# Rows of the last five expert blocks kept in SBUF, the others added onto the tokens by DMA during the last blocks

## What is computed

```
mod = silu(c) @ w_ada + b_ada                    # 9 rows: 1 prompt, 8 sample groups
sh1, sc1, g1, sh2, sc2, g2 = split(mod, 6)       # 1024 columns each
...
h2 = x * (1 + sc2) + sh2
for e in 16 experts (each token takes 2 of them, weights gate[e]):
    he = silu(h2 @ w_e_gate[e]) * (h2 @ w_e_up[e])
    y  = y + gate[e] * (he @ w_e_down[e])
x = layer_norm(ALPHA * x + (1 + g2) * y, ln2_g, ln2_b)
```

## Time and profile before

| | us |
|---|---|
| median of 3 runs | 1105.62 |
| the runs | 1103.91 to 1107.01 |
| the profiled execution | 1110.89 |
| its span, first to last instruction | 1109.0 |
| PE busy in the span | 1009.2 |
| DVE busy | 492.8 |
| ACT busy | 186.2 |
| POOL busy | 253.0 |
| mean granted TensorE clock (1 is 2.4 GHz) | 0.948 |

### The profile page before, as it was taken

The page is one execution under the profiler, slowest core; times in us unless marked ns, Lnnn a source line. Parts: engine busy times, 40 slices in busy tenths (PEclk is TensorE's granted clock), DMA queues, the critical chain, the costliest instruction groups (busy, mean ns, idle before and its releaser), DMA issues. The chain is left out here.

```text
span 1109.0 us, 22156 instructions
## 1 busy us (share of the span) xinstructions
PE 1009.2 (91%) x8966; PEld 676.4 (61%) x8966; DVE 492.8 (44%) x1281; ACT 186.2 (17%) x441; POOL 253.0 (23%) x287
## 2 busy tenths in 40 slices
PE   4999999998999999999999999987999999998930
PEld 3777777455876766667777764565655555554510
DVE  2122999972356888855104004677133011010117
ACT  2110112113122212221111110111111111111103
POOL 0000005445121113222325430000221221211133
PEclk8998999999798999999999999986999999999975
DMA  9955645452515206114081317142969899999856
GB/s 307 300 112 157 181 153 204 142 194 78 196 29 162 67 15 193 31 46 113 11 211 36 114 52 300 66 180 96 367 252 417 324 377 392 421 414 419 323 155 121
DMA packets 93733, 214.23 MB, mean 193 GB/s; under 512 B 23465, under 2 KB 48304, under 8 KB 89534
## 3 DMA queue, kind: packets, MB, share of 16 engines
q1 hardware_dynamic: 78388, 186.20, 47.0%
q0 software_dynamic: 6400, 19.01, 5.8%
q10 hardware_dynamic: 8849, 7.64, 2.5%
HBM read 200.46 MB, written 16.92 MB: 196 GB/s over the span
## 5 line engine op out<-in xcount | busy, mean ns | idle before, releaser
L1747 PE MATMUL bank<-arena 128*128 128x288 f32 (+6 forms) x1778 | 444.1, 406 | 6.5 <-issue 2.1
L1747 PEld LDWEIGHTS bank<-arena 128*128 128x128 f32 (+2 forms) x1778 | 321.3, 193 | 121.3 <-issue 45.9
L2138 PE MATMUL bank<-arena 128*32 128x256 f32 x3136 | 181.4, 382 | 8.5 <-issue 6.6
L2138 PEld LDWEIGHTS bank<-arena 128*32 128x32 f32 x3136 | 103.5, 109 | 78.4 <-issue 12.4
L1699 DVE TENSOR_TENSOR arena<-arena,bank 128x128 f32<-128x128 f32 x49 | 14.2, 289 | 229.5 <-ACT arena L1142 229.3
L914 POOL DMA_INDIRECT expert_rows<-arena,ints x49 | 47.7, 974 | 228.0 <-ACT arena L1153 228.0
L864 POOL TENSOR_SCALAR arena<-arena 128x288 f32<-128x288 f32 x48 | 45.3, 943 | 219.5 <-ACT arena L1104 219.5
L2157 PE MATMUL bank<-arena 128*32 128x256 f32 x1568 | 94.6, 381 | 0.0
L1215 DVE SCALAR_TENSOR_TENSOR arena<-arena 128x512 f32<-128x512 f32 x120 | 81.9, 741 | 0.0
L1761 PE MATMUL bank<-arena 128*128 128x288 f32 x256 | 69.2, 428 | 2.6 <-DVEq L1233 2.6
L1751 PE MATMUL bank<-arena 128*128 128x128 f32 (+7 forms) x315 | 51.7, 300 | 17.8 <-DMA arena<-constants 5.0
(11 more groups left out here) (282 smaller groups left out, 880.5 us busy)
## 6 DMA issues: line engine op xcount, KB each, us to landing
arena<-in_w_e_gate SPq DMA_DIRECT2D x16, 2048.0 KB, 11.0
arena<-in_w_e_up SPq DMA_DIRECT2D x16, 2048.0 KB, 16.3
arena<-in_w_e_down SPq DMA_DIRECT2D x16, 2048.0 KB, 21.4
arena<-in_w_ada SPq DMA_DIRECT2D x8, 2048.0 KB, 10.5
arena<-in_w_in SPq DMA_DIRECT2D x8, 2048.0 KB, 10.1
arena<-in_w_ada SPq DMA_DIRECT2D x8, 1024.0 KB, 11.6
arena<-in_x_prompt SPq DMA_DIRECT2D x8, 512.0 KB, 5.2
arena<-in_w_in SPq DMA_DIRECT2D x14, 256.0 KB, 8.2
```

What stands on the lines that cost most here:

```text
L1747: last = pe.matmul(out, a, b, start=k == 0, stop=k == len(pairs_) - 1)
L2138: last = pe.matmul(out, HG[:, g % 2, k, a:a + BLK], gate_up[i % 2][:, :, k, c * P:c * P + P], start=k == 0, stop=k == KT - 1)
```

## The change

- `y_d` and a second tensor `y2_d` (for the further rows) are set to zero at the beginning: POOL clears 128 x 512 and issues two DMAs of 1,280 rows x 4 KB from it, in step `("ada", 8)`, ahead of that step's own work.
- Only the columns of `mod` from g1 on are stored. For n of 10 and 11 (g2) POOL adds 1 to the bias first, one more instruction each.
- Per block POOL fetches the quarters of 1 + g2 that its rows need (`gate_rows`, an indirect DMA of 128 rows x 1 KB) two blocks ahead; DVE, not ACT, takes the result out of PSUM and multiplies by weight and gate in one instruction (`result_up`).
- Blocks 0 to 43 (`SENT` = 44) are scattered as before. Blocks 44 to 48 (`KEPT` = 5) stay in `YR`.
- `GAT`, its five loads and DVE's L1730 go away. In their place POOL adds `y_d` onto `X1` in SBUF with accumulating DMAs: five for the first rows, five for the second, each second one after its first has landed. They begin when block 45 is up.
- The kept blocks are added by PE: one-hot matrices built by DVE in blocks 21 to 25, then per tile 5 x 4 products of 32 x 128 by 32 x 256 into four PSUM banks; DVE's sum over the row reads `X1` and these banks.
- DVE starts the end part only after POOL's `further_added`, which follows POOL's last accumulating DMA and its 21 branch tests.
- The list of rows carries a conditioning row number with each place, decoded by a few small DVE instructions in `list_up`, `spread_up`.

```diff
+SENT = FIRST[NE - 2]
+KEPT = NBLK - SENT
...
             if kind == "ada":
                 n = key[1]
+                if n == 8:
+                    own.link(pool.memset(ZERO, 0.0))
+                    for rows in (y_d, y2_d):
+                        pool.dma_start(rows[0:2 * SLEN].rearrange("(p n) (h d) -> p (n h) d", p=P, d=512),
+                                       ZERO.unsqueeze(1).broadcast_to([P, 2 * SLEN * 2 // P, 512])).then_inc(ev("zeroed"), 16)
...
                 pool.wait_ge(ev("mod_raw"), n - 3)
                 pool.wait_ge(ev(bada_in(n)[0]), bada_in(n)[1])
+                if n >= 10:
+
+                    own.link(pool.tensor_scalar(bada_buf(n), bada_buf(n), 1.0, None, ALU.add))
                 pool.tensor_tensor(mod_buf(n), mod_buf(n), bada_buf(n), ALU.add).then_inc(ev("mod_row"), 1)
...
+        def gate_rows(d):
+
+            pool.indirect_dma_start(G2B[:, d % 2, :], None, gates, bass.IndirectOffsetOnAxis(ints[:, I_ROW + d:I_ROW + d + 1], 0)).then_inc(ev(f"g2_in{d % 2}"), 16)
+
+        def add_rows(t, second, src, sem_name):
+            a = t * P + SLEN * second
+            pool.dma_start(X1[0:rows_of(t), t, :], src[a:a + rows_of(t), :], accum_op=ALU.add).then_inc(ev(sem_name), 16)
+
+        def firsts(t):
+            add_rows(t, 0, y_d, f"pair_in{t}")
+
+        def seconds(t):
+            pool.wait_ge(ev(f"pair_in{t}"), 16)
+            add_rows(t, 1, y_d, f"pair_in{t}")
+
+        pool.wait_ge(ev("weights_up"), 1)
+        gate_rows(0)
+        gate_rows(1)
+        for d in range(NBLK - 2):
...
             pool.wait_ge(ev("yo_up"), d + 1)
-            pool.indirect_dma_start(quarters, bass.IndirectOffsetOnAxis(ints[:, I_DEST + d:I_DEST + d + 1], 0), YR[:, d % YRS, :], None).then_inc(stored(d)[0], 16)
+            if d < SENT:
+
+                pool.indirect_dma_start(quarters, bass.IndirectOffsetOnAxis(ints[:, I_DEST + d:I_DEST + d + 1], 0), YR[:, yr_of(d), :], None).then_inc(stored(d)[0], 16)
+            gate_rows(d + 2)
+            if d == SENT + 1:
+
+                for done_ in stored_by(SENT):
+                    pool.wait_ge(*done_)
+                firsts(0)
+                firsts(1)
+                seconds(0)
+        firsts(2)
+        seconds(1)
+        firsts(3)
+        seconds(2)
+        firsts(4)
+        seconds(3)
+        seconds(4)
...
+        pool.sem_inc(ev("further_added"), 1)
...
+        def result_up(d):
+
+            dve.wait_ge(ev("dn_full"), d + 1)
+            if YRS <= d < SENT:
+                dve.wait_ge(*stored(d - YRS))
+            dve.wait_ge(ev(f"g2_in{d % 2}"), 16 * (d // 2 + 1))
+            stt(YR[:, yr_of(d), :], banks[6 + d % 2][:, 0:256], WBLK[:, d:d + 1], G2B[:, d % 2, :], ALU.mult, ALU.mult).then_inc(ev("yo_up"), 1)
...
+        dve.wait_ge(ev("further_added"), 1)
+        dve.wait_ge(ev("rows2_in"), 32)
         for t in range(NT):
-            n, a, m = rows_of(t), GAT[0:rows_of(t), t, :], TOTAL[0:rows_of(t), t:t + 1]
-            dve.wait_ge(ev(f"pair_in{t}"), 16)
-            link(tt_(a, a, BC2[0:n, 0 if t < 4 else 1, :], ALU.mult))
-            link(dve.tensor_tensor_reduce(out=a, in0=a, in1=X1[0:n, t, :], scale=1.0, scalar=0.0, op0=ALU.add, op1=ALU.add, accum_out=m))
...
+            dve.wait_ge(ev(f"pair_in{t}"), 32)
+            dve.wait_ge(ev("rows_summed"), t + 1)
+            by_quarter = x.rearrange("p (c f) -> p c f", c=4)
+            link(dve.tensor_tensor_reduce(out=by_quarter, in0=by_quarter, in1=sums[0:n], scale=1.0, scalar=0.0, op0=ALU.add, op1=ALU.add, accum_out=total))
...
+        for t in range(NT):
+            n = rows_of(t)
+            if t == 1:
+                pe.wait_ge(ev("yo_up"), NBLK)
+            if t >= 2:
+                pe.wait_ge(ev("row_mean"), t - 1)
+            for k in range(KEPT):
+                if t == 0:
+                    pe.wait_ge(ev("yo_up"), SENT + k + 1)
+                for c in range(4):
+                    rows = slice(BLK * c, BLK * c + BLK)
+                    last = pe.matmul(sum_banks(t)[0:n, c, :], OHT[k][rows, t, 0:n], YR[rows, YRS + k, :],
+                                     start=k == 0, stop=k == KEPT - 1)
+            last.then_inc(ev("rows_summed"), 1)
```

More of the change, by code:

```diff
@@ L151 @@
 A_YR = A_MG
[L152 removed]
+A_HEB = A_YR + (YRS + KEPT) * 256
 A_HETB = A_HEB + 3 * P
[L154 to L156 removed]
+A_G2 = A_HETB + 2 * P
+A_OHT = [A_BC + 6 * D, A_BC + 6 * D + SLEN, A_BC + 6 * D + 2 * SLEN, A_G2 + 512, A_HOT]
+assert len(A_OHT) >= KEPT and A_OHT[3] + SLEN <= A_MG + 4 * D and A_HOT + SLEN <= A_AE
 A_BC2 = A_HG + 2 * D
[L158 removed]
+assert A_BC2 + 2 * D <= A_BC + 6 * D
 A_O = A_RING
@@ L904, in _ @@
         quarters = y_d.rearrange("r (c f) -> (r c) f", c=4)
-        for d in range(NBLK):
-            if d == 0:
-                pool.wait_ge(ev("weights_up"), 1)
+        gates = mod_d.rearrange("r (k f) -> (r k) f", f=256)
+        def gate_rows(d):
[12 more added lines that the diff above has]
+        for d in range(NBLK - 2):
             for g in range(2, TILES):
@@ L1138, in _ @@
         act.activation(HG[:, 0, 4:8, :], quarter_tiles(banks[4]), ACT.Copy).then_inc(ev("gt_b"), 1)
-        for b in range(NBLK + 2):
-            if b < NBLK:
-                act.wait_ge(ev("hid_full"), b + 1)
-                act.activation(HEB[:, b % 3, :], banks[b % 3][:, 0:P], ACT.Silu).then_inc(ev("he_silu"), 1)
+        for b in range(NBLK):
+            act.wait_ge(ev("hid_full"), b + 1)
+            act.activation(HEB[:, b % 3, :], banks[b % 3][:, 0:P], ACT.Silu).then_inc(ev("he_silu"), 1)
             if b in tile_behind:
@@ L1169, in _ @@
             act.wait_ge(ev("row_mean"), t + 1)
-            act.activation(G[0:n, t % 2, :], GAT[0:n, t, :], ACT.Square, bias=NMEAN[0:n, t:t + 1], scale=1.0 / 32, accum_out=SQUARES[0:n, t:t + 1]).then_inc(ev("last_squares"), 1)
+            act.activation(G[0:n, t % 2, :], X1[0:n, t, :], ACT.Square, bias=NMEAN[0:n, t:t + 1], scale=1.0 / 32, accum_out=SQUARES[0:n, t:t + 1]).then_inc(ev("last_squares"), 1)
             act.wait_ge(ev("last_squares"), t + 1)
@@ L2204, in _ @@
         each_further(pe, nov, further)
+        with pe.If(nov > 0):
+            pe.wait_ge(ev("further_added"), 1)
+        pe.wait_ge(ev("he_ready"), NBLK)
+        pe.wait_ge(ev("het_up"), NBLK)
+        for t in range(NT):
+            n = rows_of(t)
+            if t == 1:
[10 more added lines that the diff above has]
+            last.then_inc(ev("rows_summed"), 1)
 def buckets():
@@ L2234, in constants @@
     c[:, K_STEP:K_STEP + NOV] = np.arange(NOV)[None, :]
-    c[:, K_DEST:K_DEST + 2 * NT] = p + P * np.arange(2 * NT)[None, :] + 1
+    token = p + P * np.arange(NT)[None, :]
+    row = np.where((token >= SEQ) & (token < NTOK), (token - SEQ) // ST + 1, 0)
+    c[:, K_DEST:K_DEST + 2 * NT] = p + P * np.arange(2 * NT)[None, :] + 1 + PLACES * np.concatenate([row, row], 1)
+    c[:, K_ROW:K_ROW + 1] = 12 + p // BLK
+    c[:, K_CND:K_CND + NB] = PLACES * np.arange(1, NB + 1)[None, :]
     c[:, K_LEFT:K_LEFT + 1] = p + 2 * SLEN + 1
```

162 lines of the change are left out of this document (88 added, 74 removed).

## The result

The changed kernel takes **1129.01 us** (median of 4 runs, 1124.39 to 1130.22); beside it the kernel before took 1104.76 (1103.57 to 1107.01). The ratio is 1.0202, with a 95% interval of 1.0171 to 1.0232. The profiled execution took 1130.22, its span is 1128.3, the mean granted clock 0.946. (PE is TensorE, ACT ScalarE, DVE VectorE, POOL GpSimd, SP SyncE.) The change is longer beyond doubt; whether by more than 2% the interval leaves open.

The account below looks back on a forecast made before the run. It took PE to bound the conditioning stretch, PE and transfers the expert blocks, and a chain of landings plus DVE's tiles the end. Terms 16.6 + 4 - 1.6 = +19 on 1105.6 gave 1125 us, range 1100 to 1138.

Parts of the forecast that it names:

- Zeroing, early: Conditioning stretch: POOL's small transfers land only behind the zeros, so PE is delayed by 16.6 us (ends +8.6 and +26.6).
- L: Conditioning stretch: the time the zeros land, taken as 282 (ends 274 and 292); PE resumes at L + 6.6.
- two landings that the prediction worked out: Conditioning stretch: zeros land at 282 by its own working, or at 278 by the Trainium skill's fit.
- 10 us or more: Conditioning stretch, sign of the forecast: PE idle this long between 270 and 290.
- Blocks: Expert blocks: fetched gate rows add bytes where DMA is full, +4 us (ends 0 and 9).
- DVE seldom waits: Expert blocks: fetches are issued two blocks (11 us) ahead and land after 6.8, so DVE rarely waits for them.
- End: After the blocks: DVE starts 4.5 us later, then its tiles and tail take 6.2 less; sum -1.6 (ends -17, +7).
- small transfers aren't held up: Rival, conditioning stretch: only shared bandwidth and added POOL instructions cost, +6 there, 1114 in all; chance 0.16.
- the full overlap: Rival, end: accumulating DMAs reach the plain rate and finish with the last block, end 17 us earlier; chance 0.14.
- slow accumulation: Rival, end: accumulating DMAs into SBUF cost 3.5 us each, 1134 in all; chance 0.08.
- hidden slack: Rival, early stretch: it has unseen slack, the rest as forecast, 1105 to 1108; chance 0.08.
- serial products: Rival, end: kept blocks' products run one after another, 8.5 us per tile, 1141 in all; chance 0.04.

Follow-up runs that it names:

- no fetches: The changed kernel with gate rows fetched for blocks 0 and 1 only and reused for all others; 1124.44 us, ratio 1.0154 to the kernel before.
- the kernel with four buffers: The changed kernel with gate rows fetched four blocks ahead in four buffers instead of two; 1127.32 us, ratio 1.0196 to the kernel before.
- the second profile of before: The kernel before, unchanged, profiled once more, on the third group's chip; 1109.14 us, span 1107.3.
- mended: The changed kernel with zeroing from SP's queue, bias instructions ahead of the raw-row wait, DVE's and POOL's single tests, spread transfers; 1109.55 us, ratio 1.0023.
- the kernel with the transfers spread: The changed kernel with DVE testing for further tiles, plus accumulating DMAs spread two each at blocks 44, 45, 46, four behind; 1122.10 us, ratio 1.0145.
- one test: The kernel with the transfers spread, plus POOL's 21 branches put inside one test for further tiles; 1127.76 us, ratio 1.0182 to the kernel before.
- each fetch twice: The changed kernel with each gate-row fetch done twice, the second copy into a spare place nobody reads; 1173.37 us, ratio 1.0586.

## Why the prediction was right

It said 1125 (1100 to 1138), slower at 0.76; it is 1129.0. By its steps, on the two spans:

1. **Zeroing, early: forecast +16.6, measured +15.4 at the gates.** The assumption that small transfers land only behind the zeros held: with the zeros on another queue the 25.9 us of a bias load are 5.9, and the gates come 13.6 us earlier. L was forecast at 282 and is 280.6, and PE resumes at L + 6.8 (forecast 6.6). Of the two landings that the prediction worked out, 282 and 278, the first was nearer. PE's idle time came out at 9.56 us, a little under the "10 us or more" that was to show it. What the sum left out: POOL's added issues delayed its root, a stall of 4.86 us for PE at 256.99 (1.38 before) that was absorbed, and the clock, which is 0.50 to about 306.
2. **Blocks: forecast +4, measured +6.4** (no fetches: 303.3 us, so about 5 are theirs). The mechanism fits, bytes where the transfers are full, though no run isolates the bytes; I counted from 915, and they are full from about 900 on, with 22 fetches for 18. "DVE seldom waits" was wrong, 17 waits of 48.5 us in all, and without effect, as the kernel with four buffers shows.
3. **End: forecast -1.6, measured -2.3.** DVE starts 6.4 us later behind the last product (forecast 4.5). The last accumulating DMA is issued 1.8 us later than forecast, counted from the last product (forecast 1079.6 with it at 1063.7, that is 15.9 behind, its end at 1103.01 with 1085.3, 17.7), and from there to DVE's start it is 4.2 us where the forecast had 4.1 (3.6 for the branches and a register load). From there to the end it is 8.8 us less, not 6.2: the tail behind DVE's last instruction is 4.3 us instead of 6.9. Its cause wasn't found; it lies between 4.2 and 6.9 in all kernels here. So the agreement in this term is partly luck: the start was forecast too early by 1.9, and the tail, which the forecast took as fixed, gave 2.6 back. And the prediction's first paragraph has the last product end near 1060; it ends at 1063.70, the figure that its third part uses.

The sum of the spans is +19.3 against +19; the errors of the three terms (-1.2 at the gates, +2.4, -0.7) largely cancel. The medians differ by 24.3, since the profile of before was 5.3 over its median and that of after 1.2, and so the forecast came 4 us low. The record of the executions says where to look. The 25 executions of the kernel before in the groups of the experiments go along with the mean granted clock: the nine at 0.954 or more took 1100.8 to 1106.1 us, the eleven at 0.950 or less 1103.4 to 1113.2. The profiled one was at 0.948. Of the change's four, three are at 0.946 and 0.947 (1127.9 to 1130.2 us) and one at 0.952 (1124.4). So the two profiles are both of executions at a low clock, where the distance is 19, while the medians compare a kernel before at a higher clock with a change at a low one. That fits the 4 to 5 us; no run tests it, and why the change gets the low clock more often is open.

Of the rivals, that small transfers aren't held up fell with the change's own rows; the full overlap fell with the rate: the accumulating DMAs keep the transfers busy at 213 GB/s from 1088 to 1098, which is the rate of before and so speaks against slow accumulation too; hidden slack fell with the first block, 15.2 us late; serial products fell with 3.0 us per tile (between the 2.2 and 4.3 of the working).

**Where the expected gain went.** The change takes a chain of landings off the end. Its end is shorter by no more than 2.3 us (0.6 against the second profile of before), because DVE stands behind POOL's branch tests and twice the accumulating bytes; mended, it is 12.4 us shorter than in that second profile. The front costs 15.4, of which 13.6 are a matter of the queue, and the blocks 6.4, of which about 5 go when the fetches go: the price of gating before the scatter.

**Open.** What breaks PE's products into groups of four 1.4 us apart. It stands beside three or more indirect DMAs in a row on POOL, but the same row of DMAs was harmless at the same place (808 to 816) in the kernel with the transfers spread. The three kernels that show it most ran on another chip than that one; whether the chip or the program's layout decides wasn't tried. Nor was it asked whether PE is short of instructions there: the trace has DMAs of a kind of their own for these (queue q8, "instruction", 32 packets of 16 KB from 777 to 1030 in the change), and the profile names no wait for them. A form without fetches (the gate applied once behind the sum, with the kept rows left ungated) wasn't tried either.

## What to carry to other kernels

A large transfer put into an idle window costs what its queue's later small transfers are worth to someone; give it a queue on which nobody waits. That isn't all: small transfers on other queues also land later while the zeros are on their way (64 KB after 9.8 us instead of 1.9), so look who loads in the window, on any queue, before you choose it. When a stall disappears from one engine (DVE's 48.5 us) and the time doesn't move, look at what is full, not at who waits: here it was the transfers, at a share of 1.00 or more with and without the fetches, so that added bytes are the first suspect. And a wait that is only needed in a case that doesn't occur should stand inside the test for this case, on every engine that passes it.

## What the hardware showed beside this

- **Another queue, another order.** 18 KB behind 10.5 MB on the same queue land after 25.9 us, beside them on another after 5.9, with the DMA engines full in both; with neither it was 3.1. The other queue isn't free of them either: 64 KB on SP's queue beside zeros on POOL's took 9.8 and 10.9 us instead of 1.9 and 1.8.
- **POOL's root is slower beside DVE instructions with two operands in SBUF.** The 128x1 root (L939 before, L994 after) takes 1.24 to 1.30 us in the end part of the kernel before, 0.54 to 0.57 in that of the change but for the last tile's (1.31). POOL's timeline of the kernel before:

```profile
1087.50 1.24 POOL L939 TENSOR_TENSOR arena<-arena 128x1 f32<-128x1 f32 x1 [2.71 <-ACT arena L1173]
```

POOL's timeline of the changed kernel:

```profile
1113.04 0.54 POOL L994 TENSOR_TENSOR arena<-arena 128x1 f32<-128x1 f32 x1 [2.15 <-ACT arena L1219]
```

Beside the first, DVE works on two operands in SBUF (L1730, L1731); beside the second, the sum over the row (L1813) reads one of its two from PSUM. The slow last root of the change (1.31, at 1121.28) stands beside L1822, which reads only SBUF; and where DVE does nothing (at 1109.56 in the kernel with the transfers spread) the root takes 0.56. That fits the Trainium skill, "SBUF — State Buffer", section "Who interferes with whom": a DVE `tensor_tensor` with both inputs in SBUF contends with GpSimd's reads. No run here varies that alone, but all these rows fall on its side.
- **Branches.** A test on POOL that isn't taken costs 0.15 us in the chain that ended last (0.04 and 0.11). 21 of them make 3.3 of the 4.2 us before DVE's start; with one test around the 20 single ones, POOL is idle for 1.44 us there instead of 4.20.
- **Products in fours.** At 814 PE issues four products every 1.42 us, where it issues 64 in 3.6 us otherwise, without a wait that the profile shows. The blocks of the two kernels that show it most are 9 us (one test) and 43 us (each fetch twice) longer; how much of that such places make wasn't added up.
